# Attention on one core: the product with the values by pairs of key tiles, in two halves of PSUM's partitions

## What is computed

```
logits = jnp.einsum('bqhgd,bqkhd->bqhgk', q.astype(f32), kg.astype(f32)) * (HEAD_DIM ** -0.5)
logits = jnp.where(valid[:, :, None, None, :], logits, -jnp.inf)
p = jax.nn.softmax(logits, axis=-1)
o = jnp.einsum('bqhgk,bqkhd->bqhgd', p, vg.astype(f32))
```

## Time and profile before

| | |
|---|---|
| median of 3 runs | 3200.93 us (3200.27 to 3201.02) |
| profiled execution | 3198.51 us |
| span of its trace | 3196.7 us |
| mean granted TensorE clock | 0.983 |
| PE, DVE, ACT, POOL busy | 96%, 68%, 33%, 39% |

### The profile page before, as it was taken

The page is one execution under the profiler, slowest core; times in us unless marked ns, Lnnn a source line. Parts: engine busy times, 40 slices in busy tenths (PEclk is TensorE's granted clock), DMA queues, the critical chain, the costliest instruction groups (busy, mean ns, idle before and its releaser), DMA issues.

```text
span 3196.7 us, 54413 instructions
## 1 busy us (share of the span) xinstructions
PE 3072.6 (96%) x20484; PEld 2941.4 (92%) x20484; DVE 2173.8 (68%) x3818; ACT 1063.1 (33%) x1938; POOL 1251.2 (39%) x736
## 2 busy tenths in 40 slices
PE   5999999999999999999979999989999999999998
PEld 4999998669999999999979999976799899999998
DVE  6259998845585656774572799988446856576735
ACT  5430112750353333433244201137413433333321
POOL 2023333004637764445330233320155477644460
PEclk8999999999999999999989999989999999999999
DMA  3121224103323446754231212230133244477533
GB/s 137 54 73 40 67 94 135 34 28 123 105 99 105 145 142 212 257 191 172 99 121 60 67 47 75 93 120 27 48 119 102 91 132 144 140 248 260 177 131 109
DMA packets 164574, 369.50 MB, mean 116 GB/s; under 512 B 18528, under 2 KB 60096, under 8 KB 164416
## 3 DMA queue, kind: packets, MB, share of 16 engines
q10 hardware_dynamic: 114144, 209.45, 18.3%
q1 hardware_dynamic: 50272, 157.96, 15.4%
HBM read 261.53 MB, written 105.83 MB: 115 GB/s over the span
## 4 chain that ended last, share of the span: by engine, by line
PE 79%; DVE 11%; DMA 3%; issue 3%; ACT 2%; POOL 2%; ACTq 1%; SPq 0%; DVEq 0%; POOLq 0%
PE PS L782 25%; PE PS L1186 16%; PE PS L1251 14%; PE PS L791 8%; PE PS L865 5%; PE PS L1084 3%; PE PS L1044 2%; PE PS L1067 2%; PE PS L953 1%; PE PS L915 1%; PE PS L897 1%; DVE X L2171 1%; DVE X L2177 1%; DMA HN<-f_keep 1%; DVE HN L2126 1%
## 5 line engine op out<-in xcount | busy, mean ns | idle before, releaser
L782 PE MATMUL PS<-H,W 128*128 128x358 f32 (+1 forms) x4032 | 663.6, 327 | 0.6 <-POOL W L605 0.6
L782 PEld LDWEIGHTS PS<-H,W 128*128 128x128 f32 x4032 | 662.2, 189 | 0.7 <-POOL W L605 0.7
L603 POOL TENSOR_TENSOR W<-RAW,ones 128x1024 fp32r<-128x1024 f32 x80 | 157.4, 1968 | 880.7 <-PE PS L782 828.6
L1251 PE MATMUL PS<-FB,DW 128*128 128x268 f32 (+1 forms) x3456 | 424.4, 285 | 1.0 <-DVE FB L2741 1.0
L1251 PEld LDWEIGHTS PS<-FB,DW 128*128 128x128 f32 x3456 | 423.9, 188 | 1.4 <-POOL DW L738 1.2
L2395 DVE TENSOR_SCALAR_CACHE_REDUCE PASS<-SC,TC,CST 128x400 bf16<-128x400 f32 x372 | 356.1, 1019 | 1.7
L1186 PE MATMUL PS<-TT,WF 128*128 128x268 f32 (+1 forms) x2688 | 339.2, 285 | 0.0
L1186 PEld LDWEIGHTS PS<-TT,WF 128*128 128x128 f32 x2688 | 334.0, 188 | 0.1
L1186 PE MATMUL PS<-H,WF 128*128 128x268 f32 (+1 forms) x2016 | 259.4, 286 | 3.1 <-ACT SQ L1748 1.6
L1186 PEld LDWEIGHTS PS<-H,WF 128*128 128x128 f32 x2016 | 252.8, 189 | 4.3 <-issue 4.3
L865 PE MATMUL PS<-WQ,H 128*128 128x364 f32 (+1 forms) x1296 | 240.9, 342 | 12.2 <-POOL WQ L610 5.6
(11 more groups left out here) (256 smaller groups left out, 4943.6 us busy)
## 6 DMA issues: line engine op xcount, KB each, us to landing
RAW<-in_w_slab SPq DMA_DIRECT2D x168, 512.0 KB, 3.6
RAW<-in_w_half SPq DMA_DIRECT2D x56, 384.0 KB, 4.0
DR<-in_w_half SPq DMA_DIRECT2D x56, 384.0 KB, 3.7
FL<-f_keep ACTq DMA_DIRECT2D x18, 1072.0 KB, 10.1
FL<-f_keep ACTq DMA_DIRECT2D x18, 1056.0 KB, 10.3
f_keep<-TB ACTq DMA_DIRECT2D x48, 268.0 KB, 4.5
f_keep<-TB ACTq DMA_DIRECT2D x48, 264.0 KB, 4.4
SK<-in_w_half SPq DMA_DIRECT2D x32, 384.0 KB, 3.3
```

What stands on the lines that cost most here:

```text
L603: g_.tensor_tensor(hi, raw, one, ALU.mult).then_inc(hi_split, 1)
L782: mm = nc.tensor.matmul(PS[:, b0 + c, 0:cw], W[:, s, w, k, :], act[:, a, k, c * cw:(c + 1) * cw], start=(first and w == 0 and a == 0), sto ...
L1251: last = nc.tensor.matmul(PS[:, to + c, 0:qw], DW[s][:, w, kk - u * UNITK, :], down_act(q, a, kk, c * qw, (c + 1) * qw), start=(kk == 0 an ...
```

## The change

- From tile 1 on (a >= 2), `values` takes as its stationary operand only the 64 columns of the group's own head. Key tiles of even number write to partitions 0 to 63 of the bank, those of odd number to partitions 64 to 127. So a group's sum lies in two halves. The meta keys are multiplied with a 128-column stationary as before, whose upper 64 columns are zero (`VM` has three forms now, and is made by six small VectorE operations instead of three).
- Two neighbouring full key tiles form a batch (`BATCHES`): PE turns both tiles of the next batch, then does both products of this one. A tile without a partner and the meta keys are batches of one. `PT` has four buffers instead of three.
- `rows_at(n)` spreads a group's four rows of logits over all its batches.
- ScalarE copies both turned tiles of a batch, and then takes the exponentials.
- A finished group is collected in two moves: ScalarE copies one half of the sum to `O2` (`o_half_copy`, two operations), and VectorE adds the other half (two tensor_tensor operations in place of two copies). `outputs` now stands behind `meta_rows`.

```diff
+        BATCHES = []
+        for _u, (_a, _kv, _kt) in enumerate(STEPS):
+            paired = _a >= 2 and _kt % 2 == 1 and key_tiles(ORDER[_a])[_kt][2] == P
+            if paired:
+                BATCHES[-1].append(_u)
+            else:
+                BATCHES.append([_u])
...
+        def rows_at(n):
+
+            i, b, nb = place(n)
+            return [(j, g) for j, g in ROW_UNITS if j == i + 2 and max(g, 0) * nb // GROUP == b]
...
+                    elif a >= 2:
+                        h = kt % 2
+                        nc.tensor.matmul(PS[h * HD:(h + 1) * HD, 6 + kv, 0:GROUP * m], V[0:w, vt, kv * HD:(kv + 1) * HD],
+                                         PT[0:w, u % 4, 0:GROUP * m], start=(kt < 2), stop=False).then_inc(pv_done, 1)
...
-                for u in range(NU):
-                    for j, g in rows_at(u):
+                for n, us in enumerate(BATCHES):
+                    for j, g in rows_at(n):
                         logits(j, g)
-                    if u + 1 < NU:
-                        turn_p(u + 1)
-                    values(u)
+                    if n + 1 < len(BATCHES):
+                        for u in BATCHES[n + 1]:
+                            turn_p(u)
+                    for u in us:
+                        values(u)
...
+                def o_half_copy(i):
+
+                    a, kv = divmod(i, NKV)
+                    m = ROWS[ORDER[a]]
+                    act.wait_ge(pv_done, l * NU + ENDS[i])
+                    act.wait_ge(o_lo, l * 18 + i - 1)
+                    for odd in range(2):
+                        copy(O2[odd * HD:(odd + 1) * HD, i % 2, :, 0:m], half_of(kv, 1 - odd, m)[:, :, odd, :])\
+                            .then_inc(o_half, 1)
...
+                    if part == 0 and i > 2 * NKV:
+                        o_half_copy(i - 1)
+                    if part == 1 and i > 1:
+                        o_hi_copy(i - 2)
+                o_half_copy(NGRP - 1)
+                o_hi_copy(NGRP - 2)
+                o_hi_copy(NGRP - 1)
...
+                        if a >= 2:
+                            dve.wait_ge(o_half, (l * (NGRP - 2 * NKV) + i - 2 * NKV) * 2 + 2)
+                            o = PS[odd * HD:(odd + 1) * HD, 6 + kv, 0:GROUP * m].rearrange("p (g o m) -> p g o m", o=2, m=m)
+                            to = O2[odd * HD:(odd + 1) * HD, i % 2, :, 0:m]
+                            V_.tensor_tensor(to, to, o[:, :, odd, :], ALU.add).then_inc(o_made, 1)
+                            continue
```

More of the change, by code:

```diff
@@ L436, in build @@
         o_made, o_hi, o_lo = sem("o_made"), sem("o_hi"), sem("o_lo")
+        o_half = sem("o_half")
         pads_zero, mask0 = sem("pads_zero"), sem("mask0")
@@ L1601, in _ @@
                 behind = [(1, g) for g in range(GROUP)]
[L1602 to L1606, removed]
[L1607 to L1614 removed]
+                for n, us in enumerate(BATCHES):
+                    i, part, _ = place(n)
+                    a, t = i // NKV, ORDER[i // NKV]
+                    m = ROWS[t]
+                    if i % NKV == 0 and part == 0 and 0 < a < 7:
+                        q_load(a + 2)
+                    for u in us:
+                        w = key_tiles(t)[STEPS[u][2]][2]
+                        act.wait_ge(turned_p, l * NU + u + 1)
+                        if u >= 4:
+                            act.wait_ge(pv_done, l * NU + u - 3)
+                        if w == N_META:
+                            copy(PTR[0:NST, u % 4, 0:GROUP * m], PS[0:NST, 4 + u % 2, 0:GROUP * m]).then_inc(pt_made, 1)
+                        else:
+                            copy(PT[0:w, u % 4, 0:GROUP * m], PS[0:w, 4 + u % 2, 0:GROUP * m]).then_inc(pt_made, 1)
@@ L1615, in _ @@
                     for j, g in behind:
                         exponent(j, g)
-                    behind = [(j, g) for j, g in rows_at(u) if g >= 0]
-                    if i + 1 < len(ENDS) and u == ENDS[i + 1] + 1:
-                        o_hi_copy(i)
-                        i += 1
-                while i < 18:
-                    o_hi_copy(i)
-                    i += 1
+                    behind = [(j, g) for j, g in rows_at(n) if g >= 0]
+                    if part == 0 and i > 2 * NKV:
+                        o_half_copy(i - 1)
@@ L2525, in _ @@
                 behind = [(1, g) for g in range(GROUP)]
-                for u, (a, kv, kt) in enumerate(STEPS):
-                    i, n, rows = NKV * a + kv, len(key_tiles(ORDER[a])), rows_at(u)
+                for b in range(len(BATCHES)):
+                    rows = rows_at(b)
+                    i, part, _ = place(b)
                     for x in range(max(len(rows), len(behind), 1)):
@@ L2530, in _ @@
                             mask_row(*rows[x])
-                        if x == 0 and kt == 0 and i:
-                            outputs(i - 1)
                         if x < len(behind):
@@ L2535, in _ @@
                     behind = [(j, g) for j, g in rows if g >= 0]
-                    if u == 0:
+                    if b == 0:
                         meta_values()
-                    if kt == 0 and NKV <= i + 1 < NGRP:
+                    if part == 0 and NKV <= i + 1 < NGRP:
                         meta_rows(i + 1)
-                    if kt == min(2, n - 1) and i > 1:
+                    if part == 0 and i:
+                        outputs(i - 1)
+                    if part == 1 and i > 1:
                         o_lo_part(i - 2)
```

45 lines of the change are left out of this document (23 added, 22 removed).

## The result

The changed kernel takes 3160.93 us, the median of 4 runs (3158.77 to 3162.69), against 3200.60 for the kernel before, measured beside it (4 runs, 3195.49 to 3201.02). The ratio is 0.988, its interval 0.9867 to 0.9891: 1.2% faster, 39.7 us, where 15 were predicted and the range ended at 3169. The profiled execution took 3162.69 us, its span is 3160.6, and its mean granted clock 0.985 against 0.983.

What follows compares the result with a forecast made beforehand. PE was taken to bound the kernel, VectorE pacing tiles 1 to 3 as much. Overlap -19.2, switches +3.4, VectorE operations +0.8 make -15.0: from 3198.5 to 3183.5, plus 2.4 for the median, 3186 us; range 3169 to 3207.

Steps and rivals of the forecast that it cites:

- three more VectorE operations and the later outputs: First groups: three small VectorE operations at 0.28 us, with `outputs` placed later, add 0.4 a layer, 0.8 us in all.
- The overlap: Pairs of 64-column products in two halves: 0.43 us saved per pair, 27.5 of PE work, 19.2 on the path.
- a2 and b1: In a pair's instructions a1, a2, b1, b2, only the first product's second and second product's first overlap, saving 0.43 us.
- The rival that had this mechanism: Both products of a pair run wholly at once: -32 us, 3169; chance 0.08.
- The switches: Changes between 64-column and full-width products: 0.03 us each, 112 counted in tiles 4 to 7, 3.4 us.
- The third rival: Each width switch is a full stop of 0.20 us: +8, 3209; decides from 0.17 us a switch; chance 0.10.
- Where the work is on the path: Per-tile gains: 0 in tiles 1 and 2, then 0.6, 1.0, 2.3, 2.4, 3.3; 9.6 us a layer.
- its sign of being wrong: Tiles 1 to 4 each longer by more than a microsecond, with PE idle before its logits until a mask.
- Order of the rest: Places of exponentials, `outputs` and logits rows on the queues: spread logits counted 0, between small gain and small loss.
- Half copies: ScalarE's two 64 x 256 copies per group: 0.8 us a group, 1.6 per tile; the last covered by VectorE's wait.
- The test for tile 7: A tile 7 batch repeats every 2.2 us; 2.6 means no overlap, 1.8 full overlap, more than 2.6 full stops.
- The second test: The second product's first instruction should start within some hundredths of the first product's second instruction.

Runs made afterwards that it cites:

- the repeat: The changed kernel measured once more without any edit, beside the kernel before: 3161.10 us, ratio 0.9884.
- in one half: Changed kernel, but from tile 2 on both products of a pair write to the same half, halves changing from pair to pair: 3209.95 us.
- at 128 columns: Changed kernel's batches, order and rows, but products of 128 columns, without halves or half copies: 3188.39 us, ratio 0.9964.
- fours in one tile: Changed kernel, but tile 7's full key tiles go in batches of four: 3154.77 us, and 3156.63 us when measured again.

## Why the prediction was wrong, step by step

The first runs split the change into three parts, which add up to its whole:

| part | from, to | measured | predicted |
|---|---|---|---|
| order: batches, spread rows, places on the queues | 3198.6 to 3188.4 | -10.2 | +0.8 |
| narrow stationaries, half copies | 3188.4 to 3210.0 | +21.6 | +3.4 |
| the two halves at once | 3210.0 to 3160.9 | -49.0 | -19.2 |

(The predicted 0.8 for three more VectorE operations and the later outputs stands in the first row, since that kernel has both. The last row takes 3160.93 from other runs; the repeat gave 3161.10.) Each of the three was misjudged, and the errors cancelled in part: the sum was off by 23 us, its terms by 11, 18 and 30.

**The overlap** is the step that failed. The prediction let only a2 and b1 stand side by side, since the four instructions stand in the order a1, a2, b1, b2, and took 0.43 us of 0.86. The chip gives all of it, 0.85. Two rows of the changed kernel show how, the instructions of a pair that run between 685.4 and 685.9, and those that still run at 686.4:

```profile
685.45 0.65 PE L1098 MATMUL PS<-PT,V 128*64 128x512 f32 x2
```

```profile
685.93 0.60 PE L1098 MATMUL PS<-PT,V 128*64 128x512 f32 x2
```

Two start together, and 0.48 later the other two. One product's first instruction doesn't start 0.43 before the other's, as it would if a2 and b1 alone ran together. The trace also tells which they are: the two that start at 685.93 are the ones that count up `pv_done`, so each is the second instruction of its product. So each half goes through its own two instructions. Whether the chip takes them in the program's order and lets b1 pass the waiting a2, or issues the four already alternated, no row tells. The rival that had this mechanism was given 0.08, on the strength of that one argument. Its sum, 3169, was still 8 us too long: it had the switches at 0.03 and nothing for the order. The Trainium skill ("TensorE: Matmul & The Clock Gate", Part 3: Packing small matmuls) says that column tiles run concurrently; the trace agrees, with two products in 1.01 us instead of 1.86. Its words on starts and ends in program order, which the prediction leaned on, don't hold for these two-instruction products as the prediction read them, with the order a1, a2, b1, b2.

**The switches** were mis-sized: 0.03 each was taken, from the 48-column stationaries of the projections, and 0.15 to 0.17 was measured (0.13 as a mean over tile 7 with batches of one), near the upper bound of 0.20 from the earlier trace rows. They also cost in all tiles from 2 on, where the prediction counted only tiles 4 to 7: tile 3 is longer by 1.38 in one half than at 128 columns (18.39 against 17.01). Two things differ here from the nearest rows: the operands are float32 and not fp32r (the profile writes f32 for both), and wide and narrow alternate after 4 to 8 instructions. Which of them matters was not tried. Something that goes with the price can be seen in PEld. Before, the first weights of the next transposes are loaded under the products, here 0.43 us ahead of their matmul at 691.91:

```profile
691.48 0.14 PEld L1067 LDWEIGHTS PS<-CST,PA 128*128 128x128 f32 x1 [0.24 <-issue]
```

In the changed kernel PEld is idle for 0.81 us behind the narrow loads and begins together with its matmul (within 0.003 us behind every batch of narrow products). Whether this missing load ahead is the price, or only goes with an emptying of the array, is not shown. The Trainium skill ("TensorEngine Tiling (Array Packing)", Tiling Modes, Key Properties) says that a change of tiling mode drains the TensorE; the trace agrees that there is a cost at each change, 0.15 us. The third rival put the point of decision at 0.17 a switch, for an overlap of half; with the 21.6 measured for narrow products and half of the 49.0, the halves would have gained some 3 us. It was the full overlap that carried them.

**Where the work is on the path.** Tile 4 gained 1.4 (predicted 1.0, less 0.4 for its 12 switches), tile 5 3.5 (2.3 less 0.4), tile 6 3.6 (2.4 less 0.5), tile 7 4.6 (3.3 less 0.5): the larger overlap, less dearer switches. Tile 3 gave 2.7, not 0.6: PE is now busy for all 14.96 us of it, so VectorE at 16.6 us busy before was no floor; it is busy for 14.55 now. How much of VectorE's work falls between two ends of a tile depends on how far the rows run ahead, and reading a floor from one stretch took that for fixed. Of tile 7's 4.6, 0.4 is the shift of the cut. Tiles 1 and 2 were to give nothing and gave -0.6 and +1.7. Tile 2 thus shows what the prediction had named as its sign of being wrong, a tile over a microsecond longer with PE idle before its logits until a mask; but of tiles 1 to 4 it was the only one.

**Order of the rest**, counted at 0, was worth 10.2 us at full width; with the pairs in place the rows alone are worth 11.9. The prediction looked for it in tiles with few rows a step; it was mostly ahead of tile 1, in the groups with two batches, a stretch that it had not cut out at all (24.68 against 27.79 at full width), and 1.1 us in tile 6, which the earlier trace rows show with PE idle for 0.6, not busy all the time as the prediction had read. The order on ScalarE and the later place of the outputs were rightly called covered. What they save is now known: 4 and 5 us.

**Half copies**: 0.8 us a group predicted, 0.78 measured for the two, and from 560 to 660 us VectorE has no wait for them. At the end of the stage they are hidden, as was said: from the last meta product to the end of the program it is 906.95 us before and 906.75 after.

**The test for tile 7** was a batch of 2.2 us, with 1.8 for full overlap and 2.6 for none. It measured 2.03, between two cases, since one number held two unknowns. The second test (when does the second product start) told them apart, and it spoke for the rival.

## What to carry to other kernels

When two matmuls each need half the array's columns, put them next to each other in different halves of PSUM's partitions: with the float32 products here the second was free, but each run of narrow matmuls between wide ones cost 0.3 us, so make runs long (batches of one with the old rows lost 34 us, batches of two with spread rows won 39.7, fours in one tile 4.5 more). When steps are merged into batches, look at what else was dealt out by steps, here the rows of logits, and look first at the groups with the fewest batches. Price a new mechanism by two numbers of the trace that can be read apart, not by their sum.

## What the runs showed of the hardware

- Two float32 products of 128x64 by 512 columns, each of two instructions, take together as long as one if they write to different halves of PSUM's partitions (1.01 us with one switch, against 1.86 in one half). The first instructions of both start together, then the second ones 0.48 us later, and all four weight loads lie within 0.20 us.
- Each change between 64-column and 128-column stationaries in float32 costs 0.15 to 0.17 us (0.29 to 0.34 for a batch, 0.29 for a product alone, 0.26 as its mean over tile 7), where the 48-column stationaries of the earlier trace rows showed at most 0.03.
- In the changed kernel no weights of the next transposes are loaded under narrow products. In the kernel before they are.
- The stretch from the first logits to the end of tile 0 got 3.2 us shorter at a granted clock of 0.65 against 0.69, so the clock did not shorten it. The clock counts there too: the same changed kernel took 24.58 us at 0.65 and 23.64 at 0.71.
- Two ScalarE copies of 128x512 from PSUM one behind the other take 1.08 us, one by itself 0.60.
